# Sparse expert rows gathered whole, their sums folded by transfers, and one low split of twelve on VectorE, in a hybrid decoder layer with a product-key expert FFN

## What is computed

```python
q = (xt @ w_pq).reshape(T, PEER_HEADS, 2, PEER_HALF_DIM)
s = jnp.einsum('thpd,hpkd->thpk', q, sub_keys)
...
experts = jnp.take_along_axis(cand_i, top_pos, axis=-1)     # 8 heads x 16 = 128 experts a token
gates = jax.nn.softmax(top_s, axis=-1)
...
u = jnp.take(expert_u, eb, axis=0)
act = jax.nn.gelu(jnp.einsum('tkd,td->tk', u, xb), approximate=False)
v = jnp.take(expert_v, eb, axis=0)
return jnp.einsum('tk,tkd->td', gb * act, v)
```

## Time and profile before

| what | value |
|---|---|
| median of 3 runs | 1913.71 us (1912.99 to 1914.73) |
| span of the profiled execution | 1912.15 us; its own time isn't listed apart from the runs |
| busy in the span | TensorE 99%, its weight loads 92%, VectorE 72%, ScalarE 50%, GpSimd 73% |
| U stage | 571.3 to 1251.25 us, gate stage from 852.15 us |
| V stage | from 1251.25 us, last piece at 1896.38 us |
| data moved | 448 MB, of it 367 MB by SyncE's queue, 67 MB by GpSimd's |

### The profile page before, as it was taken

The page is one execution under the profiler, slowest core; times in us unless marked ns, Lnnn a source line. Parts: engine busy times, 40 slices in busy tenths (PEclk is TensorE's granted clock), DMA queues, the critical chain, the costliest instruction groups (busy, mean ns, idle before and its releaser), DMA issues.

```text
span 1912.2 us, 35061 instructions
## 1 busy us (share of the span) xinstructions
PE 1896.7 (99%) x11798; PEld 1758.9 (92%) x11798; DVE 1383.4 (72%) x2585; ACT 950.5 (50%) x1342; POOL 1390.8 (73%) x708
## 2 busy tenths in 40 slices
PE   9999999999999999999999999999999999999997
PEld 7888889888999999999999999999999999999997
DVE  7534684045545777968888888479889889999986
ACT  6453355475544444544444444455555555555555
POOL 3867768887998999998888888976555525666711
PEclk9999999999999999999999999999999999999999
DMA  8544546564655666666666566689999988999984
GB/s 307 186 143 153 199 144 224 193 190 155 218 188 177 207 209 208 210 202 196 194 192 196 189 195 195 200 280 351 333 336 334 333 297 298 337 325 334 328 273 145
DMA packets 128380, 448.29 MB, mean 234 GB/s; under 512 B 16528, under 2 KB 19472, under 8 KB 127632
## 3 DMA queue, kind: packets, MB, share of 16 engines
q1 hardware_dynamic: 102240, 367.29, 58.5%
q0 software_dynamic: 20480, 67.13, 10.0%
q10 hardware_dynamic: 5584, 12.88, 2.0%
HBM read 443.04 MB, written 4.19 MB: 234 GB/s over the span
## 4 chain that ended last, share of the span: by engine, by line
PE 72%; POOL 17%; issue 8%; DMA 1%; DVE 1%; ACT 0%; POOLq 0%; SPq 0%; DVEq 0%; ACTq 0%
PE ps L1885 22%; PE ps L1982 22%; POOL wlo L438 17%; PE ps L1888 12%; PE ps L1985 11%; PE ps L1899 1%; PE ps L1585 1%; PE ps L1587 1%; PE ps L1586 1%; PE ps L1961 1%; DMA raw<-in_w_front 0%; PE ps L1869 0%; DMA big<-in_x_t 0%; PE ps L1963 0%; ACT whi L539 0%
## 5 line engine op out<-in xcount | busy, mean ns | idle before, releaser
L438 POOL TENSOR_TENSOR wlo<-raw,whi 128x1024 fp32r<-128x1024 f32 x436 | 1057.6, 2430 | 207.9 <-ACT whi L539 193.1
L539 ACT ACTIVATE whi<-raw 128x1024 fp32r<-128x1024 f32 x435 | 461.2, 1060 | 633.7 <-PE ps L1888 361.8
L1885 PE MATMUL ps<-x_parts,whi 128*128 128x448 f32 x2048 | 588.9, 369 | 0.0
L1982 PE MATMUL ps<-gate_parts,whi 128*128 128x448 f32 x1992 | 573.6, 369 | 0.0
L734 ACT ACTIVATE whi<-raw 128x1024 fp32r<-128x1024 f32 x256 | 271.7, 1061 | 294.9 <-PE ps L1985 255.8
L1888 PEld LDWEIGHTS ps<-x_parts,wlo 128*128 128x128 f32 x2048 | 384.7, 188 | 31.3
L1985 PEld LDWEIGHTS ps<-gate_parts,wlo 128*128 128x128 f32 x1992 | 374.2, 188 | 30.8
L1888 PE MATMUL ps<-x_parts,wlo 128*128 128x224 f32 x2048 | 386.9, 270 | 0.0
L1985 PE MATMUL ps<-gate_parts,wlo 128*128 128x224 f32 x1992 | 376.0, 270 | 0.0
L1437 DVE TENSOR_TENSOR wlo<-raw,whi 128x1024 fp32r<-128x1024 f32 x248 | 303.9, 1225 | 68.1 <-ACT whi L734 52.1
L1885 PEld LDWEIGHTS ps<-x_parts,whi 128*128 128x128 f32 x2048 | 310.3, 191 | 0.0
(11 more groups left out here) (266 smaller groups left out, 2217.2 us busy)
## 6 DMA issues: line engine op xcount, KB each, us to landing
raw<-in_w_u SPq DMA_DIRECT2D x256, 512.0 KB
raw<-in_w_v SPq DMA_DIRECT2D x256, 512.0 KB
raw<-in_w_front SPq DMA_DIRECT2D x180, 512.0 KB
big<-in_mem ACTq DMA_DIRECT2D x8, 256.0 KB, 5.6
big<-in_mem_t ACTq DMA_DIRECT2D x2, 1024.0 KB, 6.2
big<-in_x ACTq DMA_DIRECT2D x2, 1024.0 KB, 7.3
x_back<-x2t_scratch ACTq DMA_DIRECT2D x2, 896.0 KB
big<-in_x_t SPq DMA_DIRECT2D x3, 512.0 KB, 8.4
```

Of the source, the lines that this page charges most:

```text
L438: nc.gpsimd.tensor_tensor(wlo[:, j % SPL, :], raw[:, j % RAW, :], whi[:, j % SPL, :], ALU.subtract).then_inc(lo_done, 1)
L539: nc.scalar.activation(whi[:, j % SPL, :], raw[:, j % RAW, :], ACT.Copy).then_inc(hi_done, 1)
L1885: nc.tensor.matmul(sums[:, 0:2 * TD], whi[:, s, cols], x_parts[:, :, m, 0:TD], start=m == 0, stop=False, skip_group_check=True)
L1982: nc.tensor.matmul(sums[:, 0:2 * TD], whi[:, s, cols], gate_parts[:, g, :, 0:TD], start=False, stop=False, skip_group_check=True)
```

## The change

Sparse part: a partition is now one of 4 slot groups times one of 32 tokens, and holds the whole row of 2048 columns. 32 gathers of U and 32 of V, each 128 x 8 KB, go into a ring of 3. The first three are issued by GpSimd between its low splits of V pieces 3 to 7. Sums over columns are complete in a partition, so that the fold by matmul at piece 121 goes; the output of the four groups is added at the end by transfers that bring the partitions of groups 1 to 3 to those of group 0, and adds over 32 partitions. The residual of these tokens is the fourth addend. The picks are made per slot group, and sum in PSUM. U's low split of piece 10 in each body of 12 is VectorE's, behind the join of pieces 6 and 7.

```diff
-TD, TS, PARTS, PD = 224, 32, 4, 512
+GROUPS = 4
+TS = P // GROUPS
+PER = -(-P // GROUPS)
-RING = 12
+RING = 3
-POOL_END = V0 + 8
-FOLD_BODY, LAST_ROWS = 10, 242
+FOLD_BODY = 10
-def issued_u(d):
-    return OPENING if d < RING else taken_u(d - RING) + 1
-def taken_u(d):
-    return 15 + d * 41 // 50
-def issued_v(e):
-    return 117 + e if e < RING else taken_v(e - RING) + 1
-def taken_v(e):
-    return 132 + e * 21 // 25
+ROWS_FROM, WEIGHTS_AT_PIECE, ROWS_UNTIL = 15, 127, 234
+ADDED_AT = (*range(240, 239 + GROUPS), 251)
+def taken(n):
+    if n < PER:
+        return ROWS_FROM + n * (WEIGHTS_AT_PIECE - 6 - ROWS_FROM) // PER
+    return WEIGHTS_AT_PIECE + 1 + (n - PER) * (ROWS_UNTIL - WEIGHTS_AT_PIECE) // PER
+def issued(n):
+    return 3 + n if n < RING else taken(n - RING) + 2
+U_VECTOR = 10
...
# GpSimd
+            with pool.Fori(U0 // BODY, U0 // BODY + U_BODIES) as i:
+                for j in range(BODY):
+                    if j != U_VECTOR:
+                        rest_of(i * BODY, j)
...
+            for j in range(2 * NK):
+                if j < OPENING:
+                    rest_of_v(j)
+                if j == 3:
                     pool.wait_ge(picks, 1)
+                while asked < 2 * PER and j >= issued(asked):
+                    gather(asked)
+                    asked += 1
...
# ScalarE, V pieces 3 to 11
+                if j == 3:
+                    for g in range(GROUPS):
+                        act.dma_start(X_S[g * TS:(g + 1) * TS, :], x2_dram).then_inc(x_s_in, 16)
+                if j == 6:
+                    act.dma_start(X_GAINED, gain_rows[0].partition_broadcast(P)).then_inc(gain_s_in, 16)
...
# ScalarE, V piece 125
+                if j == 5:
+                    act.wait_ge(rows_taken, PER)
+                    nc.scalar.activation(WEIGHTS, SUMS, ACT.Gelu, scale=PICK_R).then_inc(sparse_gelu, 1)
...
# ScalarE, body 19 (V pieces 228 to 239)
+                if j == 8:
+                    act.wait_ge(rows_taken, 2 * PER)
+                    load_addend(0)
+                    load_addend(1)
...
# ScalarE, body 20 (V pieces 240 to 251)
+                if j == 3:
+                    for k in range(2, GROUPS):
+                        act.wait_ge(group_added, k - 1)
+                        load_addend(k)
+                    act.wait_ge(group_added, GROUPS - 1)
+                    act.dma_start(ADDEND[GROUPS], gain_rows[1].partition_broadcast(TS)).then_inc(last_gain_s_in, 16)
...
# VectorE, in join
+                if c % CHUNKS_PER_BODY == U_VECTOR // 2 - 2:
+                    n = 2 * c + 4
+                    dve.wait_ge(hi_done, k0 * 2 + (U0 + n + 1))
+                    nc.vector.tensor_tensor(wlo[:, (U0 + n) % SPL, :], raw[:, n % RAW, :], whi[:, (U0 + n) % SPL, :],
+                                            ALU.subtract).then_inc(lo_u_done, 1)
...
+            def row_taken(n):
+                dve.wait_ge(row_in[n % RING], 16 * (n // RING + 1))
+                row, k = ROW[n % RING], n % PER
+                weight = WEIGHTS[:, k:k + 1]
+                if n < PER:
+                    ins = nc.vector.tensor_tensor_reduce(row, row, X_GAINED, 1.0, 0.0, ALU.mult, ALU.add, SUMS[:, k:k + 1])
+                elif k == 0:
+                    ins = nc.vector.tensor_scalar(X_GAINED, row, weight, None, ALU.mult)
+                else:
+                    dve.wait_ge(rows_taken, n)
+                    ins = nc.vector.scalar_tensor_tensor(X_GAINED, row, weight, X_GAINED, ALU.mult, ALU.add)
+                ins.then_inc(rows_taken, 1)
+            def add_group(k):
+                dve.wait_ge(group_in[k], 16)
+                if k:
+                    dve.wait_ge(group_added, k)
+                nc.vector.tensor_tensor(Y_S, Y_S, ADDEND[k], ALU.add).then_inc(group_added, 1)
...
+                if j in ADDED_AT:
+                    add_group(ADDED_AT.index(j))
+                if j == 252:
+                    dve.wait_ge(group_added, GROUPS)
+                    step(nc.vector.tensor_tensor_reduce(ADDEND[GROUPS - 1], Y_S, Y_S, 1.0, 0.0, ALU.mult, ALU.add,
+                                                        stats[0:TS, SPARSE_R:SPARSE_R + 1]))
...
-            nc.vector.scalar_tensor_tensor(X_GAINED, X_S, stats[:, R + N_LAST:R + N_LAST + 1], LAST_GAIN_S,
+            nc.vector.scalar_tensor_tensor(Y_S, Y_S, stats[0:TS, R + N_LAST:R + N_LAST + 1], ADDEND[GROUPS],
...
# TensorE, picks
-            for k, src in enumerate((CH[:, 0, last], CH[:, 1, last], GE[:, last], stats[:, R + N_X2 + 1:R + N_X2 + 2])):
-                w = P if k < 3 else 1
-                ins = nc.tensor.matmul(ps[:, 7, k * P:k * P + w], SEL, src, start=True, stop=True)
+            for k, src in enumerate((CH[:, 0, last], CH[:, 1, last], GE[:, last])):
+                for g in range(GROUPS):
+                    w = min(PER, P - g * PER)
+                    nc.tensor.matmul(ps[:, 7, k * PER:k * PER + w], SEL[:, g, :], src[:, g * PER:g * PER + w],
+                                     start=g == 0, stop=g == GROUPS - 1, skip_group_check=True)
+            for g in range(GROUPS):
+                ins = nc.tensor.matmul(ps[:, 7, 3 * PER:3 * PER + 1], SEL[:, g, :], stats[:, R + N_X2 + 1:R + N_X2 + 2],
+                                       start=g == 0, stop=g == GROUPS - 1)
...
# TensorE, V piece 121, and before the third piece from the end
-                    pe.wait_ge(rows_taken, P)
-                    for b in range(2):
-                        ins = nc.tensor.matmul(ps[:, b, 2 * TD:512], FOLD, SUMS[:, b * 64:(b + 1) * 64],
-                                               start=False, stop=False, skip_group_check=True)
...
-            nc.tensor.matmul(ps[:, 2, 2 * TD:2 * TD + 1], FOLD, stats[:, SPARSE_R:SPARSE_R + 1],
-                             start=False, stop=False, skip_group_check=True).then_inc(norm_folded, 1)
```

339 lines of the change are left out of this document (152 added, 187 removed).

## The result

The changed kernel takes 1939.6 us (median of 4 runs, 1939.3 to 1940.5) against 1913.4 us beside it: ratio 1.0139, 95% interval 1.0125 to 1.0154. It is slower by 26 us. The span of its profiled execution is 1938.7 us, 26.5 more than before; that execution took 1940.5.

A forecast was written before the change was run, and what follows sets the result against it. TensorE, busy 99% of the span, was taken as the bound; terms 2.0 + 11.0 + 3.6 + 1.0 + 1.2 + 4.1 + 0.9 + 1.6 - 0.5 = +24.9 on 1913.7 gave 1938.6 us, range 1922 to 1951.

The forecast's parts named there:

- Folds removed: TensorE no longer does the fold matmuls: gain 0.5 us; the lighter row work on VectorE and GpSimd gains nothing.
- Picks: Twelve selections of 32 columns and four of one, at 0.185 and 0.14 us each, cost TensorE +2.0 us.
- The split in the gate stage: VectorE's U low split shifts its later gate work 1.59 us; TensorE loses about 1.0 a body, +11.0 over 11.
- The rival of absorbed work: The gate stage hides the moved split, so the term of 11 goes: 1927.6 us; chance 0.12.
- the port rival: GpSimd's splits hold VectorE's new split up to 2.4 us more in each of 11 bodies: up to 1965; chance 0.03.
- Opening: Start of V: three gathers among GpSimd's low splits, 3.75 us less slack of 0.2, delay TensorE by +3.6 us.
- traffic: Opening of V: 5 MB of loads and gathers beside the weight stream push weights back, +1.0 us (0 to 6).
- the rival of bytes on GpSimd: GpSimd's gather time grows with bytes, +8.7 us in the opening; with late weights as alternative, 1943 to 1953, chance 0.07.
- The row at piece 128: VectorE's first V row stands ahead of the first blocks' joins, for which TensorE waits: +1.2 us (0.3 to 1.8).
- Group sums: VectorE's adds at V pieces 240 to 242 make piece 243 late by 4.1 us; work at 251 and 252 adds 0.9.
- End: The last scaling of the sparse rows, directly ahead of the eight last joins, grows to about 2.35 us: +1.6 us.
- The rival of no loss: Slack at U's bank and V's opening suffices, third transfer is timely: 1916.8 us, within 0.2%; chance 0.06.

The follow-up runs named there:

- Experiment 2: Changed kernel with VectorE's U low split at piece 2 of each body in place of piece 10: 1933.9 us, 1.0108 of the kernel before.
- experiments 3 and 4: Changed kernel with first three gathers behind GpSimd's eight low V splits: 1935.9 us; that plus four loads spread and gain rows loaded in the gate stage: 1935.4 us.
- experiment 10: Changed kernel with the first V row taken at piece 131 instead of 128 and the last scaling behind the eight joins: 1936.4 us (1.0113).
- experiment 6: Changed kernel without the three transfers that bring groups 1 to 3 to group 0, the adds kept: 1936.5 us (1.0127).

## Why the prediction was right, and where its terms were off

The mechanism was right at nearly every place. That the total came so near (1938.6 forecast, 1939.6 measured) is in part luck, as terms cancelled: the gate stage was 2.6 us smaller than said and the late weights 2.5 larger. Two falls of the clock, 1.57 and 1.58 us, and 0.95 us of GpSimd's closing drain weren't in the sum at all; the piece behind the third add was 1.4 us less late than said, the adds at 251 and 252 cost 0.7 less, the scaling 0.6 less, and the front stages were 0.7 us shorter by chance.

*Folds removed: right.* The fold's 0.37 us at V 121 went, and 0.09 at V 122 (0.5 forecast, with the small one near the end); relief of VectorE and GpSimd gave nothing.

*Picks: right in kind, 2.0 against 2.67.* The step that failed is the price of 0.185 and 0.14 a matmul, taken from pairs that stood alone. In a row each took about 0.22, the one-column ones too. And a cost was missing: the clock behind them, 1.57 us where it fell.

*The split in the gate stage: right in place and mechanism, 11.0 against 8.38.* The shift was 1.60 as forecast and the late one-hot row 0.31 (0.25 to 0.35 foretold). What failed is "Nothing earlier in VectorE's row of work gives the shift back". The same two instructions of mid-body, first before the change and then after it:

```profile
979.39 0.86 DVE L1376 SCALAR_TENSOR_TENSOR hot_rows<-iota,i_table,ps 128x256 fp32r<-128x256 bf16 x2
980.37 0.42 DVE L1382 TENSOR_TENSOR hot_row<-iota,ps 128x256 fp32r<-128x256 bf16 x1
```

```profile
986.57 0.87 DVE L1424 SCALAR_TENSOR_TENSOR hot_rows<-iota,i_table,ps 128x256 fp32r<-128x256 bf16 x2
987.34 0.43 DVE L1430 TENSOR_TENSOR hot_row<-iota,ps 128x256 fp32r<-128x256 bf16 x1
```

980.37 - 979.39 = 0.98 us before, 987.34 - 986.57 = 0.77 after: a gap of 0.2 us, too short to be marked (by the code VectorE waits there for TensorE's gate product), took up part of the shift. An earlier pair of the body took 0.07 more. At the chunk product 1.33 of the 1.60 are left (988.28 - 979.58 = 8.70 against 981.30 - 972.33 = 8.97), so that it is late by 1.33 - 0.66 = 0.67 in place of 0.93. The forecast also read only this bank; the one before, with 1.01 us of slack, was late too, which costs no more in sum. With 0.10 behind it a body comes to 0.80, where 1.0 was charged. Experiment 2 shows that the term hangs on the place alone. The rival of absorbed work didn't come about, nor the port rival: the split took its plain 1.23 us.

*Opening: GpSimd's part right (3.6 against 3.03), traffic too small (1.0 against 3.47).* Gathers of four times the bytes cost GpSimd the same 0.95 to 1.15 us, so the low end was the right one, and the rival of bytes on GpSimd falls. The term's range was 0 to 6; in the nine profiles with this opening V 7 to 12 lost 3.0 to 6.3 us, where what is above 3.5 is the clock behind the waits. I had read one wait of 2.95 us without loss as slack; experiments 3 and 4 show that the loss hangs on what falls together there.

*The row at piece 128: right,* 1.2 against 1.02, shown by experiment 10.

*Group sums: near in sum (4.1 and 0.9 against 4.57 and 0.18), off inside.* Piece 243 lost 2.69 us, not 4.1 (its terms, 2.3 + 1.22 + 0.38 less 0.3, give 3.6; for the 0.5 of waits no row stood): the transfer was issued at 1881.06, while ScalarE still worked on its piece, where I had it behind that work. The 1.68 of piece 244 are the clock behind that wait (1.58), which the forecast didn't have, and the 0.10 behind any wait. ScalarE's queue did catch up, as said. The adds cost 1.33 by themselves (experiment 6), and for those at 251 and 252 the lead of 2.2 us (2.1 by its own terms) nearly sufficed.

*End: near in number, 1.6 against 1.88, off inside.* The scaling took 2.34 as said, but delayed TensorE's last sums by 1.0 us and not by all of its added 1.6: before the change they had run back to back, and the joins had a lead. The step that failed is that these joins, as they run without a gap, pass all of it on. The other 0.95 us are GpSimd's closing drain, of which nothing was foretold.

*The rival of no loss* needed slack of 1.6 and 3.75 us at two places; TensorE waited at both.

## What to carry to other kernels

Where one engine is busy all the time, costs of the others are read as slack at each hand-over, not as busy time: the same 1.22 us instruction cost 0.76 us a body at one place and nothing 8 us later. Work is best moved to where an engine idles waiting for the busy one, and ahead of nothing that the busy one needs. And larger transfers save instructions, but they are to be paced: 5 MB bunched beside a weight stream cost 3.0 to 6.3 us, and with 1 MB of it moved away and the rest spread over some 15 pieces none in that stretch. And behind a wait like that of piece 243 an otherwise full TensorE may run on at half its clock, which here cost 1.6 us more than the wait.
